# Delta rule's inverse on four quarters of TensorE's array, its factor updates regrouped on VectorE

## The reference

```python
decay = jnp.exp(jnp.where(incl, g[..., :, None] - g[..., None, :], -jnp.inf))
k_beta = k * beta[..., None]
m = jnp.where(strict, jnp.einsum('bhnid,bhnjd->bhnij', k_beta, k) * decay, 0.0)
t_inv = lax.linalg.triangular_solve(m + eye, jnp.broadcast_to(eye, m.shape), left_side=True, lower=True, unit_diagonal=True)
...
def chunk_step(s, xs):
    qk_c, q_c, k_c, u_c, w_c, a_c = xs
    v_new = u_c - jnp.einsum('bhik,bhkv->bhiv', w_c, s)
    o_c = jnp.einsum('bhik,bhkv->bhiv', q_c, s) + jnp.einsum('bhij,bhjv->bhiv', qk_c, v_new)
    s = s * a_c[..., None, None] + jnp.einsum('bhik,bhiv->bhkv', k_c, v_new)
    return s, o_c
```

## Time and profile before

| | us |
|---|---|
| median of 3 runs | 4131.1 (4126.62 to 4139.81) |
| the profiled execution, its own time | 4129.49 |
| its span, first to last instruction | 4127.7 |
| mean granted clock of PE | 0.98 |
| PE busy | 3920.5 |
| DVE busy | 1676.7 |
| ACT busy | 857.3 |
| POOL busy | 687.2 |

### The profile page before, as it was taken

The page is one execution under the profiler, slowest core; times in us unless marked ns, Lnnn a source line. Parts: engine busy times, 40 slices in busy tenths (PEclk is TensorE's granted clock), DMA queues, the critical chain, the costliest instruction groups (busy, mean ns, idle before and its releaser), DMA issues. The chain is left out here.

```text
span 4127.7 us, 52003 instructions
## 1 busy us (share of the span) xinstructions
PE 3920.5 (95%) x21139; PEld 2417.0 (59%) x21139; DVE 1676.7 (41%) x3136; ACT 857.3 (21%) x1679; POOL 687.2 (17%) x509
## 2 busy tenths in 40 slices
PE   7998899999999999999999999989999999999988
PEld 4565545555448666588845767767656545434333
DVE  2347342233764564443374556543244314111111
ACT  3214320000121333210113333331123201100000
POOL 0003212222420111033242323220003200000000
PEclk9998999999999999999999999999999998999999
DMA  5107611112541110164253111003300416999999
GB/s 178 41 1 274 222 49 62 61 47 102 173 139 57 36 42 26 62 232 171 98 183 71 27 32 29 22 33 116 113 1 1 164 44 252 411 421 422 422 421 364
DMA packets 323236, 580.16 MB, mean 141 GB/s; under 512 B 58700, under 2 KB 189228, under 8 KB 322360
## 3 DMA queue, kind: packets, MB, share of 16 engines
q1 hardware_dynamic: 323000, 576.83, 38.1%
HBM read 566.15 MB, written 10.63 MB: 140 GB/s over the span
## 5 line engine op out<-in xcount | busy, mean ns | idle before, releaser
L3391 PE MATMUL dn_ps<-room,dn_w 128*128 128x512 f32 (+1 forms) x616 | 230.4, 520 | 0.5 <-DVE dn_v_tok L3941 0.3
L972 PE MATMUL ffn_up_ps<-room 128*128 128x384 f32 (+1 forms) x704 | 203.9, 432 | 0.0
L972 PE MATMUL ffn_up_ps<-ffn_up_t,room 128*128 128x384 f32 (+1 forms) x704 | 196.7, 432 | 0.0
L4957 PE MATMUL experts_ps<-experts_ring,experts_xs 128*64 128x512 f32 (+1 forms) x768 | 162.4, 573 | 25.1 <-DMA experts_ring<-in_w_up 25.1
L2679 PE MATMUL hgrn_ps<-room,hgrn_w 128*128 128x512 f32 x372 | 170.4, 593 | 1.4 <-DVE hgrn_v L2934 1.0
L4957 PE MATMUL experts_ps<-experts_ring,room 128*64 128x512 f32 (+1 forms) x768 | 161.0, 570 | 8.7 <-DMA experts_ring<-in_w_up 8.1
L972 PEld LDWEIGHTS ffn_up_ps<-ffn_up_t,room 128*128 128x128 f32 x704 | 133.8, 190 | 55.7
L972 PEld LDWEIGHTS ffn_up_ps<-room 128*128 128x128 f32 x704 | 133.7, 190 | 55.8
L1058 DVE TENSOR_TENSOR room<-ffn_up_ps,room 128x384 f32<-128x384 f32 (+1 forms) x154 | 73.5, 489 | 222.1 <-PE ffn_up_ps L972 220.6
L5051 DVE TENSOR_TENSOR x_sb<-x_sb,experts_ps 128x512 f32<-128x512 f32 x56 | 38.5, 688 | 298.0 <-PE experts_ps L4892 298.0
L3391 PEld LDWEIGHTS dn_ps<-room,dn_w 128*128 128x128 f32 x616 | 112.9, 192 | 76.2 <-issue 66.7
(11 more groups left out here) (699 smaller groups left out, 7355.1 us busy)
## 6 DMA issues: line engine op xcount, KB each, us to landing
experts_ring<-in_w_gate SPq DMA_DIRECT2D x128, 704.0 KB, 14.4
experts_ring<-in_w_up SPq DMA_DIRECT2D x128, 704.0 KB, 17.8
experts_ring<-in_w_down SPq DMA_DIRECT2D x160, 512.0 KB, 12.4
att_wm<-in_mod_w SPq DMA_DIRECT2D x20, 2048.0 KB, 9.1
ffn_w<-in_ffn_w_down SPq DMA_DIRECT2D x37, 1024.0 KB, 4.9
ffn_up_wm<-in_ada_w SPq DMA_DIRECT2D x12, 2048.0 KB, 12.6
ffn_w<-in_ffn_w_up SPq DMA_DIRECT2D x22, 1024.0 KB, 7.6
ffn_front<-in_ffn_w_down SPq DMA_DIRECT2D x18, 1024.0 KB, 4.9
```

Of the source, the lines that this page charges most:

```text
L972: mm = nc.tensor.matmul(result(n, p), lhs[:, k, :], rhs[:, k, :], start=k == 0, stop=k == half - 1)
L3391: mm = nc.tensor.matmul(out, ahead.tile[:, k, :] if k < by_ahead else wt[:, h % 2, piece, k, :], hT[:, k, tok], start=k == 0, stop=k == KD ...
L4957: mm = nc.tensor.matmul(ps[out_rows, 3 * n + c, 0:b - a], xs_now[:, j, at:at + SLOTS], ring[:, w_at + a:w_at + b], start=j == 0, stop=j == ...
```

## The change

Each chunk with an odd number works with its two halves exchanged, so that its products use the two off-diagonal quarters of the array.

- `y_of` writes odd chunks to the other half of the partitions and to bank 3 in place of bank 2. Y is kept by parity.
- LT of the odd chunks has to lie on the other half too. POOL makes LT only for the even chunks now; the new function `crossed` on DVE makes the odd ones, in two instructions of 64 partitions each, last in the period but for tap 4. `d_of` waits for both.
- `d_of` puts both groups into banks 3 and 4, by parity of the chunk, side by side, and signals once at the end of the second; `place_z` waits for that.
- `y_of` uses bank 3, so it waits until `place_w` of the period before has read it (`w_cp`), and in period 0 for the copy into T (`t_off`).
- `place_w` goes ahead of tap 3 of the convolution. In period 5 the copy into T is four instructions instead of two.

```diff
+        def split_of(bank, side, c, after=0):
+            return ps[sides_of[side], bank + c % 2, (after + c // 2) * BLOCK:(after + c // 2 + 1) * BLOCK]
+        def half_at(side, c):
+            return side if c % 2 == 0 else 1 - side
...
             def y_of(n, h):
                 pe.wait_ge(S["r_done"], L * h + n + 1)
                 if n == 0:
                     pe.wait_ge(S["y_out"], L * h)
+                    pe.wait_ge(S["t_off"], 2 * h)
+                pe.wait_ge(S["w_cp"], (L - 1) * h + n)
                 for c in range(TILES):
                     for side, rows in enumerate(sides_of):
                         to_side = side if n < L - 1 else 1 - side
-                        mm = nc.tensor.matmul(block_of(2, to_side, c), neg_m[rows, c, sides_of[to_side]], R[rows, c, :], start=True, stop=True)
+                        mm = nc.tensor.matmul(split_of(2, half_at(to_side, c), c), neg_m[rows, c, sides_of[to_side]], R[rows, c, :], start=True, stop=True)
...
             def d_of(n, h):
                 pe.wait_ge(S["y_out"], L * h + n + 1)
                 pe.wait_ge(S["lt_done"], L * h + n + 1)
-                if n < L - 1:
-                    for c in range(TILES):
-                        for side, rows in enumerate(sides_of):
-                            mm = nc.tensor.matmul(block_of(3, side, c), LT[rows, c, :], Y[rows, c, :], start=True, stop=True)
-                    mm.then_inc(S["d_mm"], 1)
+                pe.wait_ge(S["lt_crossed"], 2 * (L * h + n + 1))
                 pe.wait_ge(S["w_cp"], (L - 1) * h + n)
                 if n == 0:
                     pe.wait_ge(S["t_off"], 2 * h)
+                if n < L - 1:
+                    for i in range(ODD):
+                        for c in (2 * i, 2 * i + 1):
+                            for side in range(2):
+                                rows = sides_of[half_at(side, c)]
+                                nc.tensor.matmul(split_of(3, side, c), LT[rows, c, :], Y[rows, c % 2, c // 2, :], start=True, stop=True)
+                    for i in range(ODD):
+                        for c in (2 * i, 2 * i + 1):
+                            for side in range(2):
+                                rows = sides_of[half_at(side, c)]
+                                mm = nc.tensor.matmul(split_of(3, side, c, ODD), Y[rows, c % 2, c // 2, :], LT[rows, c, :], start=True, stop=True)
+                    mm.then_inc(S["dt_mm"], 1)
+                    return
                 for c in range(TILES):
-                    for side, rows in enumerate(sides_of):
-                        to_side = side if n < L - 1 else 1 - side
-                        mm = nc.tensor.matmul(block_of(4, to_side, c), Y[rows, c, :], LT[rows, c, :], start=True, stop=True)
+                    for side in range(2):
+                        rows = sides_of[half_at(side, c)]
+                        mm = nc.tensor.matmul(split_of(3, 1 - side, c), Y[rows, c % 2, c // 2, :], LT[rows, c, :], start=True, stop=True)
                 mm.then_inc(S["dt_mm"], 1)
...
-                nc.gpsimd.tensor_tensor(LT[:, :, :], W[:, h % 2, :, :], small(SMALL_HALVES + n + 1), ALU.mult).then_inc(S["lt_done"], 1)
+                nc.gpsimd.tensor_tensor(LT[:, 0::2, :], W[:, h % 2, 0::2, :], small(SMALL_HALVES + n + 1, ODD), ALU.mult).then_inc(S["lt_done"], 1)
...
-                dve.wait_ge(S["d_mm"], (L - 1) * h + n + 1)
-                nc.vector.copy_predicated(Z[:, :, :], small_mask(n + 1), blocks(3)).then_inc(S["z_cp"], 1)
+                dve.wait_ge(S["dt_mm"], L * h + n + 1)
+                nc.vector.copy_predicated(by_parity(Z[:, :, :]), parity_mask(n + 1), split_blocks(0)).then_inc(S["z_cp"], 1)
...
+            def crossed(n, h):
+                if n:
+                    dve.wait_ge(S["w_cp"], (L - 1) * h + n)
+                else:
+                    dve.wait_ge(S["w_start"], 2 * h + 2)
+                    if h:
+                        dve.wait_ge(S["dt_mm"], L * h)
+                for side, rows in enumerate(sides_of):
+                    nc.vector.tensor_tensor(LT[sides_of[1 - side], 1::2, :], W[rows, h % 2, 1::2, :], small(SMALL_HALVES + n + 1, ODD, rows), ALU.mult).then_inc(S["lt_crossed"], 1)
...
                 place_z(n, hi)
                 right(n + 1, hi)
+                place_w(n, hi)
                 if fills in ("k", "v"):
                     conv(fills, hp, 3)
-                place_w(n, hi)
...
                 carry(n, hc)
+                if n < L - 1:
+                    crossed(n + 1, hi)
+                else:
+                    crossed(0, hp)
                 if fills in ("k", "v"):
                     conv(fills, hp, 4)
```

More of the change, by code:

```diff
@@ L3207, in chunk @@
         return slice(at, at + P)
+    ODD = TILES // 2
     sides = []
@@ L3252, in delta_mixer @@
         LT = sb("LT", TILES, BLOCK)
-        Y = sb("Y", TILES, BLOCK)
+        Y = sb("Y", 2, ODD, BLOCK)
         T = sb("T", 2, 2, TILES, P)
@@ L3286, in delta_mixer @@
         block, S = stack.enter_context(phase(nc, tag, "const_in", "ab_in", "triangle_in", "w_in*6", "ab_mm", "ab_out", "gates", "gates_act", "g_done", "sums_mm", "sums_exp", "neg_done",
-                                             "side", "y_mm", "d_mm", "dt_mm", "ks_mm", "tr_mm", "su_mm", "o_mm",
+                                             "side", "y_mm", "dt_mm", "ks_mm", "tr_mm", "su_mm", "o_mm",
                                              "padded", "raw", "tap0", "k_silu", "k_sq", "v_silu", "q_silu", "q_sq", "k_turned", "dec_out", "z_start", "y_out", "wd_out", "w_out", "to_out",
@@ L3290, in delta_mixer @@
                                              "conv", "z_cp", "r_done", "w_cp", "w_start", "kk_out", "mt_done", "qk_out", "ssq_out", "ssk_out", "v_scaled", "b_done", "q_scaled", "rho", "s_done",
-                                             "o_half", "o_done", "w_ident", "lt_done", "rhs_done", "b_wide", "qk_masked", "t_done", "t_off", "stored", "z_in*2", "z_mm", "z_taken", "z_stored*4", also=[ahead.sem]))
+                                             "o_half", "o_done", "w_ident", "lt_done", "lt_crossed", "rhs_done", "b_wide", "qk_masked", "t_done", "t_off", "stored", "z_in*2", "z_mm", "z_taken", "z_stored*4", also=[ahead.sem]))
         def wide(first):
@@ L3310, in block_of, with split_blocks, by_parity, parity_mask @@
             return ps[sides_of[side], bank, c * BLOCK:(c + 1) * BLOCK]
-        def small(n):
-            return cst[:, HALVES + n // 2, n % 2 * BLOCK:(n % 2 + 1) * BLOCK].unsqueeze(1).broadcast_to([P, TILES, BLOCK])
+        def split_of(bank, side, c, after=0):
+            return ps[sides_of[side], bank + c % 2, (after + c // 2) * BLOCK:(after + c // 2 + 1) * BLOCK]
+        def split_blocks(after):
+            return ps[:, 3:5, after * BLOCK:(after + ODD) * BLOCK].rearrange("p o (c i) -> p o c i", c=ODD)
+        def by_parity(x):
+            return x.rearrange("p (c o) i -> p o c i", o=2)
+        def parity_mask(level):
+            n = SMALL_EITHER + level
+            rows = cst[:, HALVES + n // 2, n % 2 * BLOCK:(n % 2 + 1) * BLOCK]
+            return rows.bitcast(U32).unsqueeze(1).unsqueeze(1).broadcast_to([P, 2, ODD, BLOCK])
+        def half_at(side, c):
+            return side if c % 2 == 0 else 1 - side
+        def small(n, count=TILES, part=slice(0, P)):
+            return cst[part, HALVES + n // 2, n % 2 * BLOCK:(n % 2 + 1) * BLOCK].unsqueeze(1).broadcast_to([part.stop - part.start, count, BLOCK])
         def small_mask(level, part=slice(0, P)):
@@ L3658, in y_out @@
                 act.wait_ge(S["y_mm"], L * h + n + 1)
-                nc.scalar.copy(Y[:, :, :], blocks(2)).then_inc(S["y_out"], 1)
+                nc.scalar.copy(Y[:, :, :, :], ps[:, 2:4, 0:ODD * BLOCK].rearrange("p b (c i) -> p b c i", c=ODD)).then_inc(S["y_out"], 1)
             def take(n, h):
@@ L3863, in place_w @@
                     dve.wait_ge(S["w_cp"], (L - 1) * h + n)
-                    nc.vector.copy_predicated(W[:, h % 2, :, :], small_mask(n + 1), blocks(4)).then_inc(S["w_cp"], 1)
+                    nc.vector.copy_predicated(by_parity(W[:, h % 2, :, :]), parity_mask(n + 1), split_blocks(ODD)).then_inc(S["w_cp"], 1)
                     return
@@ L3867, in place_w @@
                 for d, rows in enumerate(sides_of):
-                    nc.vector.tensor_copy(T[rows, h % 2, d, :, sides_of[1 - d]], blocks(4)[rows, :, :]).then_inc(S["t_off"], 1)
+                    for odd in range(2):
+                        ins = nc.vector.tensor_copy(T[rows, h % 2, d, odd::2, sides_of[1 - d]], ps[rows, 3 + odd, 0:ODD * BLOCK].rearrange("p (c i) -> p c i", c=ODD))
+                    ins.then_inc(S["t_off"], 1)
+            def crossed(n, h):
+                if h is None or n == L:
+                    return
+                if n:
[6 more added lines that the diff above has]
```

(1 more changed line is left out.)

## The result

The changed kernel takes 4142.48 us (median of 20 runs, 4138.20 to 4148.39), the kernel before, on the same chip, 4133.98 (20 runs, 4126.62 to 4139.89): 8.5 us more, a ratio of 1.0019 with a 95% interval of 1.0013 to 1.0025. The prediction said 1 us less. It is inside the range and within 0.3%, but no measurement of "no change": the change costs something, and the prediction has no term for it.

A forecast was written before the change was run, and what follows sets the result against it. PE was taken as the bound by very little, busy 64.42 of a head's 65.66 us. Five steady heads at -4, the second about 0, the first +3 and the last +0.3 gave -1: 4130 us, range 4108 to 4150.

The forecast's parts named there:

- Part 1: PE's inverse products: four array quarters work at once, y 0.49 us, both updates 0.84, 5.95 off a head.
- Rival (a): PE quarters sharing rows don't work at once: 24 records stay at 0.84 us, 1.8 to 1.9 more a head, 4149; 22%.
- Parts 2 and 3: place_z waits for both groups yet starts 0.96 us after the updates; y(3) waits 0.64 for W, period 2 starts 1.5 sooner.
- Part 4: DVE's crossings take turns with POOL's masks: tap 4 of k 1.42 us later, su(3) 0.83, tr(5) 0.2.
- Rival (b): DVE's crossings run one behind the other, not in turns with POOL: a head gains 1.9 us, total 4120; 13%.
- The sum: Over all heads: a steady head -0.8 us, five such -4, second about 0, first +3, last +0.3, together -1.
- Rival (c): PE's gain comes through as waits are shorter: up to 47.6 us, 4083.5, more likely 4107 to 4115; 15%.

The follow-up runs named there:

- e1: The changed kernel with idle products on PE where it waits in periods 1, 3 and 5: 4132.90 us, ratio to before 0.9997.
- e5: The changed kernel with five idle products on PE in period 3 alone, none in periods 1 and 5: 4134.01 us, ratio 0.9996.
- e2: The changed kernel with the odd chunks' LT made on POOL, behind its own half factor, instead of on DVE: 4105.91 us, ratio 0.9930.
- e3: The kernel before with DVE making the odd chunks' LT, not exchanged; products stay on two quarters: 4155.56 us, ratio 1.0052.
- e6: The changed kernel with nine idle products on PE in periods 1 and 5, none in period 3: 4141.88 us, ratio 1.0019.
- e4: The changed kernel with W's update moved back behind tap 3 of the convolution: 4142.28 us, ratio 1.0024.

## Why the prediction was right and wrong

**Part 1, right.** y 0.49 forecast, 0.51 measured; both updates 0.84 and 0.86. Four quarters do work at once, two of them on the rows of the other two. Rival (a) falls with it: 0.84 us would have stayed. The Trainium skill (TensorE: Matmul & The Clock Gate, "What overlaps and what doesn't") says that a load overlaps products in flight only on other rows. The 0.51 measured here doesn't agree, and the measurement decides.

**Parts 2 and 3, right.** In period 1 place_z starts 1.00 behind the updates (2543.53 and 2542.53; 0.96 forecast). y(3) waits 0.63 for W (0.64 forecast), 4.97 behind ks, as DVE's chain had it (4.9). Period 2 starts 26.40 us into a head where nothing lowers the clock (e1; 2483.60 - 2457.20) and 27.93 before: 1.53 sooner, 1.5 forecast.

**Part 4, right in size.** The crossings took turns with POOL's masks. The timeline of DVE and POOL in the changed kernel, beside the earlier trace rows:

```profile
2559.48 2.61 POOL L3830 TENSOR_TENSOR dn_qk<-dn_s,cst 128x512 f32<-128x512 f32 x2 [0.23 <-DVE dn_s L3994]
...
2560.02 2.29 DVE L3917 TENSOR_TENSOR dn_LT<-dn_W,cst 64x192 f32<-64x192 f32 x2
2562.34 1.02 DVE L3874 SCALAR_TENSOR_TENSOR dn_kT<-x_sb,dn_taps,dn_kT 128x772 f32<-128x772 f32 x1
...
2589.43 0.74 DVE L3917 TENSOR_TENSOR dn_LT<-dn_W,cst 64x192 f32<-64x192 f32 x2
```

Two crossings take 0.74 alone (0.36 each was taken) and 2.29 between the masks; tap 4 ends 10.29 behind ks (10.3 forecast), su(3) comes 13.91 behind it (13.25 in the earlier trace rows, so 0.66 later; 0.83 forecast). Rival (b) falls. In period 5 the wait came in two places: the last update stood 1.21 for the crossing, which the prediction had not named, and tr 0.60 for rho, where it said over a microsecond.

**The sum, wrong by one absent term.** The prediction noted that the head ran "at the full clock (1.00 of 2.4 GHz)", took every duration from there, and ended with PE's busy time falling by some 40 us "while the span stands". It counted PE's new waits as lost gain and nothing more. But behind those of period 3 PE fell to half clock for 3.4 us and longer, and that cost 1.6 us (at 0.97) to 3.1 us (at 0.95) in each head from the third to the sixth: 66.2 to 67.8 in place of e5's 64.6 and 64.7. Over the four that is 10.4 us; the medians of the two kernels, each against the kernel before on its own chip, differ by 10.2. So the clock accounts for the whole loss.

With the clock held in these heads they gain 1.0 each (0.8 forecast), the second 0.4 (0), and e5 stands 1.7 us below before by its median, by its interval between 5.4 below and 2.1 above, where 1 below was forecast. Part of that agreement is luck. The first head loses 2.8 (3 forecast), but at 0.97; a fall of that size cost 1.6 in a steady head, so by that estimate the crossings hold only 1.2 of it. The seventh, which was to gain 0.8, is 2.1 longer than before, and 2.2 in e5, at 0.95 in both. Why its clock falls there was not tried.

**Rival (c)** gave 4107 to 4115 for a gain that comes through. With the crossing on DVE it does not come through. e2 shows what was in the way, at full clock: 64.6 to 61.5 us a head, of which 1.66 at su(3) (40.32 in e1, 38.66 in e2, from the head's start) and 1.3 more by tr(5) (57.80 and 54.82). These are the two places, masks and T, that Part 4 named.

## What to carry to other kernels

Where PE is the bound by a hair, shorter products turn into waits, and short waits can cost more than their length (here up to 3.1 us behind waits of 1.9 in all): look at the granted clock of the stretch behind them, and price its fall as a case of its own. If filling the wait with idle products gains time, and the same products cost time where there is no wait, it was the clock; then shorten the chain that makes PE wait, which here gained more than the filling. Where the instructions of two engines take turns, as DVE's and POOL's did here, try an added step on the one whose own later work should come second.

## What the runs showed that was not expected

- Short waits were enough for half clock. Behind waits of 0.37, 0.68 and 0.18 us in period 3 it fell; in e3 some 0.3 and 0.18 were all that stood there; in the kernel before, with no wait at the same place, these heads stayed at 1.00. The longer waits of periods 1 and 5 (1.52 and 1.21) matter less: e5 keeps them and its third to sixth heads stay at 1.00, and e6 fills them without effect. But behind the 1.52 it fell in one head of e2 and two of e4. So the length of a wait alone doesn't decide, and what does is not shown. What PE runs around the waits of period 3 are small products, 64x64 blocks and 12 records of one column; whether that matters was not tried. The Trainium skill (TensorE: Matmul & The Clock Gate, "A second HAM failure mode: psum-queue depth-cycling") tells of a kernel whose clock swings because PE pauses briefly and often between groups of products. The changed kernel's traces agree: 0.51 behind four waits of 0.18 to 0.68 us.
- Four quarters of 64x64 give a record every 15 ns (0.86 us for 48 less 0.51 for 24), half of the 29 on two.
- More work on POOL made DVE's chain shorter: in e2 POOL is busy 28.5 us a head in place of 19.3, and tap 4 of k took 1.02 us in place of the 2.06 in the earlier trace rows, because the masks came behind it.
